# The first stage rewritten: modulation weights as the standing operand, first norms and first products in one order of work

## The reference, cut to what matters

```python
mod = jnp.split((jax.nn.silu(c) @ w_ada[l] + b_ada[l])[:, None, :], N_MOD, axis=-1)
mod_c = jnp.split(jax.nn.silu(c_ctx) @ w_ada[l] + b_ada[l], N_MOD, axis=-1)
...
h_lat = _modulate(_rmsnorm(x, norm1_g[l]), sh1, sc1)      # x: 1024 latent tokens
h_ctx = _modulate(_rmsnorm(ctx, norm1_g[l]), sh1c, sc1c)  # ctx: 256 context tokens
... = jnp.split(h_lat @ w_in, offs, axis=-1)              # and h_ctx @ w_in
```

## Time and profile before

| | us |
|---|---|
| median of 3 runs | 3436.4 (3435.8 to 3438.77) |
| profiled execution | 3435.87, its span 3434.6 |
| TensorE busy | 3270.4 (95%) |
| VectorE busy | 1929.5 (56%) |
| ScalarE busy | 1373.2 (40%) |
| POOL busy | 384.1 (11%) |
| mean granted clock | 0.98 |

### The profile page before, as it was taken

The page is one execution under the profiler, slowest core; times in us unless marked ns, Lnnn a source line. Parts: engine busy times, 40 slices in busy tenths (PEclk is TensorE's granted clock), DMA queues, the critical chain, the costliest instruction groups (busy, mean ns, idle before and its releaser), DMA issues. The chain is left out here.

```text
span 3434.6 us, 39599 instructions
## 1 busy us (share of the span) xinstructions
PE 3270.4 (95%) x14862; PEld 2659.9 (77%) x14862; DVE 1929.5 (56%) x3098; ACT 1373.2 (40%) x2320; POOL 384.1 (11%) x605
## 2 busy tenths in 40 slices
PE   6999999989999999999999999999788899999998
PEld 3888888877788878888888888877555678888886
DVE  4474343454334387777545555655576487777443
ACT  4592232224333244333233356554576343333221
POOL 0121000001100200000010101111211100001011
PEclk8999999999999999999999999999899899999999
DMA  5365433344553423333763433444844523334752
GB/s 218 107 218 183 142 126 123 123 156 157 200 161 117 138 71 117 109 115 118 248 203 97 154 119 137 136 157 150 171 96 104 184 92 117 105 116 165 248 179 77
DMA packets 228045, 494.14 MB, mean 144 GB/s; under 512 B 21520, under 2 KB 84624, under 8 KB 226320
## 3 DMA queue, kind: packets, MB, share of 16 engines
q1 hardware_dynamic: 147728, 302.30, 27.7%
q0 software_dynamic: 80128, 189.30, 16.9%
HBM read 353.63 MB, written 137.89 MB: 143 GB/s over the span
## 5 line engine op out<-in xcount | busy, mean ns | idle before, releaser
L290 PE MATMUL p<-s_xh,s_wh 128*128 128x512 f32 x2256 | 905.6, 401 | 36.9 <-DVE s_tmp L401 12.3
L291 PE MATMUL p<-s_xl,s_wh 128*128 128x512 f32 x2256 | 888.7, 394 | 0.0
L292 PE MATMUL p<-s_xh,s_wl 128*128 128x512 f32 x2256 | 888.2, 394 | 0.0
L290 PEld LDWEIGHTS p<-s_xh,s_wh 128*128 128x128 f32 x2256 | 430.9, 191 | 131.5 <-issue 20.2
L292 PEld LDWEIGHTS p<-s_xh,s_wl 128*128 128x128 f32 x2256 | 429.6, 190 | 92.3
L291 PEld LDWEIGHTS p<-s_xl,s_wh 128*128 128x128 f32 x2256 | 430.6, 191 | 89.6 <-issue 1.7
L2092 PE MATMUL p<-s_xh,s_wh 128*128 128x512 f32 x1152 | 449.5, 390 | 1.1 <-DVE s_xl L2199 1.0
L2094 PE MATMUL p<-s_xh,s_wl 128*128 128x512 f32 x1152 | 448.3, 389 | 0.0
L2093 PE MATMUL p<-s_xl,s_wh 128*128 128x512 f32 x1152 | 448.2, 389 | 0.0
L250 DVE TENSOR_TENSOR s_wl<-s_ws,s_wh 128x1024 fp32r<-128x1024 f32 x157 | 195.3, 1257 | 235.0 <-ACT s_wh L242 234.8
L2092 PEld LDWEIGHTS p<-s_xh,s_wh 128*128 128x128 f32 x1152 | 216.3, 188 | 47.7 <-issue 2.7
(11 more groups left out here) (380 smaller groups left out, 5099.8 us busy)
## 6 DMA issues: line engine op xcount, KB each, us to landing
d_h<-s_fhl POOLq DMA_DIRECT2D x80, 512.0 KB, 3.4
s_ws<-i_Wf SPq DMA_DIRECT2D x48, 512.0 KB, 4.3
s_qb<-i_Wf SPq DMA_DIRECT2D x40, 512.0 KB, 4.1
s_qb<-i_Wf SPq DMA_DIRECT2D x80, 256.0 KB, 3.1
s_ws<-i_Wf SPq DMA_DIRECT2D x80, 256.0 KB, 2.8
s_aw<-i_adaT SPq DMA_DIRECT2D x32, 512.0 KB, 3.7
s_xh<-d_h POOLq DMA_DIRECT2D x16, 1024.0 KB, 12.0
s_xl<-d_h POOLq DMA_DIRECT2D x16, 1024.0 KB, 15.7
```

The lines of the kernel that those rows point to most:

```text
L290: pe.matmul(o, wh, H[:, k, c:c + n], start=(k == 0), stop=False)
L291: pe.matmul(o, wh, L[:, k, c:c + n], start=False, stop=False)
L292: last = pe.matmul(o, wl, H[:, k, c:c + n], start=False, stop=(k == 7))
```

## The change

- `ada_pe`: the weight tile is the standing operand, 16 blocks of 128 columns per k, and the pair of vectors moves (2 columns). Each product writes its own two columns of bank 0 (32 per k); one reduction on VectorE adds the eight up. Row copies and transposes go.
- SP: vector pair and context first, then the tiles of `w_ada` with the four weight tiles between them, then x by halves of 256 KB (all of half 0 before half 1), then `cb`, `WA0`, `cmask` and two more weight tiles. Weight tiles 2 and 3 go to `ACC` and `RB` in place of `WS`, so they need no slot given back.
- The squares of the latent halves have buffers of their own, in the place of `w_ada` tiles, so their first waits for the last of `ada_pe`. They are interleaved on ScalarE with the context's high parts. POOL adds them up.
- TensorE: column sums and spreads of the halves are put into `products_pe` by `mids` (half 0 in the context's group before k = 5 and 7, half 1 in half 0's group before k = 2 and 4). The three groups run in stage 0, and stage 1 begins with the filling products. Half 1's spread is copied to `RB`.
- The banks of the three groups change. The context's keys are copied to `ACC` and stored from there, after POOL's adds.
- `cb` and `WA0` are processed after the second group on ScalarE.

The diff, cut to its core:

```diff
+    ADA = alloc(top, [128, 32], F, "ada")
...
+    def raw_weights(i):
+
+        n = cols_of[i]
+        if 2 <= i < 4:
+            return (ACC, RB)[i - 2][:, 0:n], early_in[i - 2].at(1)
+        return WS[:, i % NS, 0:n], w_in[i % NS].at(i // NS + 1 if i < 2 else i // NS)
...
-            if i >= NS:
+            if i >= 4:
...
+        DIAG = alloc(p0, [128, 1280], F, "diag")
+        DIA = {"c": DIAG[:, 0:256], 0: DIAG[:, 256:768], 1: DIAG[:, 768:1280]}
+
+        adf = AD[:, :, :].rearrange("p a b -> p (a b)")
+        TF = TMP[:, :, :].rearrange("p a b -> p (a b)")
+        SQ = {"c": [TF[:, 256 * k:256 * k + 256] for k in range(8)],
+              0: [adf[:, 8192 + 1024 * k + 512:8192 + 1024 * k + 1024] for k in range(8)],
+              1: [adf[:, 1024 * k + 512:1024 * k + 1024] for k in range(8)]}
...
+        column_bank, spread_bank = {"c": 6, 0: 6, 1: 4}, {"c": 4, 0: 5, 1: 3}
...
-            loads = {2: (0, 1), 3: (2, 3), 4: (4, 5), 5: (6, 7)}
-            for k in range(8):
-                sp.dma_start(AD[:, k, :], D["ada"][k]).then_inc(*ad_in[k].up())
-                if k == 2:
-                    sp.dma_start(XC[:], D["ctxT"]).then_inc(*xc_in.up())
-                for x in loads.get(k, ()):
-                    sp.dma_start(RES[:, x, :], D["xT"][x]).then_inc(*x_in[x].up())
-            weights_sp(NW)
...
-        def ada_pe(k):
-            PEW.wait_ge(*silu.at(1))
-            PEW.wait_ge(*ad_in[k].at(1))
-            for c in range(4):
-                last = pe.matmul(B[c][0:2, :], sc2[:, k, :], AD[:, k, c * 512:c * 512 + 512], start=(k == 0), stop=(k == 7))
-            last.then_inc(*ada.up())
...
-            for k in range(5):
-                ada_pe(k)
-            columns_pe("c")
-            ada_pe(5)
-            spread_pe("c", [])
-            ada_pe(6)
-            columns_pe(0)
-            columns_pe(1)
-            ada_pe(7)
-            spread_pe(0, [rooted.at(1)])
-            spread_pe(1, [rooted.at(2)])
-            PEW.wait_ge(*mcopy.at(4))
-            PEW.wait_ge(*ident_in.at(1))
-            for m in range(16):
-                last = pe.transpose(B[0][:, 2 * m:2 * m + 2], mrow[:, m * 128:m * 128 + 128], ident[0:2, 0:2])
-            last.then_inc(*mturn.up())
-
...
-            for j in range(20):
-                squares_act(j)
-            root("c")
-            for j in range(20, 24):
-                squares_act(j)
-            root(0)
-            root(1)
-            weights_act(NS)
-            ACW.wait_ge(*ada.at(8))
-            for c in range(4):
-                ac.activation(mrow[:, c * 512:c * 512 + 512], B[c][0:2, :], ACT.Copy).then_inc(*mcopy.up())
-            weights_act(NW)
-            modulated_act("c")
-            modulated_act(0)
...
-            for j in range(20):
-                squares_dve(j)
-            inverse_dve("c")
-            for j in range(20, 24):
-                squares_dve(j)
-            inverse_dve(0)
-            inverse_dve(1)
-            weights_dve(NS)
-            mp = B[0][:, 0:32].rearrange("p (m j) -> p j m", j=2)
-            DVW.wait_ge(*mturn.at(1))
-            dv.tensor_tensor(MOD[:, 0:16], mp[:, 0, :], bada, ALU.add).then_inc(*mods.up())
-            dv.tensor_tensor(MODC[:, 0:16], mp[:, 1, :], bada, ALU.add).then_inc(*mods.up())
-            DVW.wait_ge(*mods.at(2))
-            dv.scalar_tensor_tensor(out=GS[:, 0:8], in0=MOD[:, 8:16], scalar=1.0, in1=n1, op0=ALU.add, op1=ALU.mult).then_inc(*mods.up())
-            dv.scalar_tensor_tensor(out=GS[:, 8:16], in0=MODC[:, 8:16], scalar=1.0, in1=n1, op0=ALU.add, op1=ALU.mult).then_inc(*mods.up())
-            DVW.wait_ge(*mods.at(4))
-            modulated_dve("c")
-            weights_dve(NW)
-            modulated_dve(0)
...
+        bank_free[0] = [mods.at(1)]
+        for b in (1, 2, 3):
+            bank_free[b] = []
         firsts = []
         for part, (col, half, n, x, ready) in enumerate(parts(True)):
+            if part == 1:
+                bank_free[6], bank_free[7] = [rooted.at(2)], []
+            if part == 2:
+                bank_free[4], bank_free[5], bank_free[3] = [rooted.at(3)], [shifted.at(16)], [spread_copied.at(1)]
             group = []
             for g, (name, m) in enumerate((("al", 0), ("k", 0), ("k", 1), ("k", 2))):
-                b = ((0, 1, 2, 3), (0, 4, 6, 7), (1, 2, 3, 5))[part][g]
+                b = ((0, 1, 2, 3), (6, 7, 1, 2), (0, 4, 5, 3))[part][g]
                 p = job(name, m, b, col, n, half, x, ready)
                 if name == "al":
                     p.ev = al_lo.at(part + 1)
...
+        def sp_():
+            sp.dma_start(sc2[:], D["cc"]).then_inc(*cc_in.up())
+            sp.dma_start(XC[:], D["ctxT"]).then_inc(*xc_in.up())
+            sp.dma_start(VEC[:], D["vec"]).then_inc(*vec_in.up())
+            sp.dma_start(ident[:], D["ident"]).then_inc(*ident_in.up())
+            for k in range(8):
+                if k in (4, 6):
+                    weights_sp(k - 2)
+                sp.dma_start(AD[:, k, :], D["ada"][k]).then_inc(*ad_in[k].up())
+            for h in range(2):
+                for k in range(8):
+                    sp.dma_start(RES[:, k, 512 * h:512 * h + 512], D["xT"][k][:, 512 * h:512 * h + 512]).then_inc(*x_in[(h, k)].up())
+            sp.dma_start(cb[:], D["crow"]).then_inc(*cb_in.up())
+            sp.dma_start(WA0[:], D["walpha"]).then_inc(*wal_in.up())
+            sp.dma_start(cmask[:], D["cmask"]).then_inc(*cm_in.up())
+            weights_sp(NW + NS)
+
+
+        def ada_pe(k):
+            PEW.wait_ge(*silu.at(1))
+            PEW.wait_ge(*ad_in[k].at(1))
+            for m in range(16):
+                c = 32 * k + 2 * m
+                last = pe.matmul(B[0][:, c:c + 2], AD[:, k, 128 * m:128 * m + 128], sc2[:, k, :], start=True, stop=True)
+            last.then_inc(*ada.up())
...
+        def spread_pe(what):
+            PEW.wait_ge(*diag.at(which[what] + 1))
+            if what == 1:
+                PEW.wait_ge(*spread3_free)
+            pe.matmul(B[spread_bank[what]][:, 0:size[what]], ones[:], DIA[what], start=True, stop=True).then_inc(*spread.up())
+
+        def pe_():
+            for k in range(8):
+                ada_pe(k)
+                if k == 1:
+                    columns_pe("c")
+                if k == 3:
+                    spread_pe("c")
+            products_pe(firsts[0], {5: lambda: columns_pe(0), 7: lambda: spread_pe(0)})
+            products_pe(firsts[1], {2: lambda: columns_pe(1), 4: lambda: spread_pe(1)})
+            products_pe(firsts[2])
...
+        def square_act(what, k):
+            ACW.wait_ge(*(xc_in if what == "c" else x_in[(what, k)]).at(1))
+            if what != "c" and k == 0:
+                ACW.wait_ge(*ada.at(8))
+            ac.activation(SQ[what][k], source(what, k), ACT.Square).then_inc(*squares.up())
...
+        def act_():
+            ACW.wait_ge(*cc_in.at(1))
+            ac.activation(sc2[:, :, :], sc2[:, :, :], ACT.Silu).then_inc(*silu.up())
+            for k in range(8):
+                square_act("c", k)
+            root_act("c")
+            weights_act(NW)
+            for k in range(8):
+                high_act("c", k)
+                square_act(0, k)
+            for k in range(4):
+                square_act(1, k)
+            root_act(0)
+            for k in range(4, 8):
+                square_act(1, k)
+            for k in range(4):
+                high_act(0, k)
+            al_act(0)
+            ACW.wait_ge(*w_lo.at(3))
+            for g, p in enumerate(firsts[0][1:]):
+                ACW.wait_ge(*p.mm)
+                ac.activation(ACC[:, 256 * g:256 * g + 256], B[p.bank][:, 0:256], ACT.Copy).then_inc(*evA.up())
+            for k in range(4, 8):
+                high_act(0, k)
+            root_act(1)
+            ACW.wait_ge(*spread.at(3))
+            ACW.wait_ge(*w_lo.at(4))
+            ac.activation(RB[:, 0:512], B[spread_bank[1]][:, :], ACT.Copy).then_inc(*spread_copied.up())
+            for k in range(8):
+                high_act(1, k)
+            al_act(1)
+            for p in firsts[1][1:]:
+                fill_act_first(p)
+            ACW.wait_ge(*wal_in.at(1))
+            ac.activation(WAL[:, :, :], WA0[:, :, :], ACT.Copy).then_inc(*wal_hi.up())
+            ACW.wait_ge(*cb_in.at(1))
+            ac.activation(cb[:, :], cb[:, :], ACT.Silu).then_inc(*cb_silu.up())
+            al_act(2)
+            for p in firsts[2][1:]:
+                fill_act_first(p)
...
+            inverse_dve("c")
+            weights_dve(NW)
+            sums = ADA[:, :]
+            DVW.wait_ge(*ada.at(8))
+            dv.tensor_reduce(sums, B[0][:, 0:256].rearrange("p (k c) -> p c k", k=8), AX.X, ALU.add).then_inc(*mods.up())
+            mp = sums.rearrange("p (m j) -> p j m", j=2)
+            DVW.wait_ge(*mods.at(1))
+            dv.tensor_tensor(MOD[:, 0:16], mp[:, 0, :], bada, ALU.add).then_inc(*mods.up())
+            dv.tensor_tensor(MODC[:, 0:16], mp[:, 1, :], bada, ALU.add).then_inc(*mods.up())
```

(123 more changed lines are left out.)

231 lines of the change are left out of this document (78 added, 153 removed).

## The result

The changed kernel takes 3459.8 us in the median of four executions (3459.3 to 3461.7) where the kernel before takes 3436.1 (3435.3 to 3438.8): a ratio of 1.0072, 95% interval 1.0059 to 1.0085. It is slower, as forecast, but by 23.7 us instead of 8.4, and above the range of 3437 to 3455. The profiled execution took 3459.89 us with a span of 3458.6, 24.0 more than the span before.

The account below looks back on a forecast made before the run. TensorE, busy 95% of the span, was taken as the bound. Sums, turn, context and latent groups move the third group's end from 127.2 to 135.6 us: +8.4, forecast 3445 us, range 3437 to 3455.

Parts of the forecast that it names:

- What follows: Everything after the third group of first products: claimed to do the same work in the same way, so no change.
- Term 1: Modulation sums: 256 weight loads at the lower clock, 0.215 us each, 55.0 us for eight tiles, from 10.0 to 66.7 us.
- The sign "a granted 0.5": Modulation sums: the granted clock was to show 0.5 until about 73 us.
- Term 2: From the sums to the first context product: 2.8 us with a 0.5 us reduction, so TensorE starts at 69.5 us.
- Term 3: Context's products: about 5 us at the lower clock, then the upper; 0.9 us wait for POOL; end at 86.0 us.
- Term 4: Latent halves' products: waits of 1.2 and 2.0 us, third group's end at 135.6 us including a clock allowance.
- the 0.8 us for the clock: Latent groups: allowance for two close waits bringing the clock down, a third of 2.3 us.
- The first: Rival on the modulation sums: clock rises, loads run 3.9 us a tile, -13.9 us in all, 3422 us; chance 0.16.
- The second: Rival on context and latent groups: POOL's adds take 1.80 us, waits lower the clock twice; +15.7, 3452 us; chance 0.12.
- The third: Rival on context and latent groups: the forecast waits do not appear; +3.5, 3439.9 us; chance 0.11.
- all three waits: TensorE's forecast waits: 0.9 us for POOL in the context group, then 1.2 and 2.0 us at the first latent half.

Follow-up runs that it names:

- e11: The kernel after, unchanged, run again on the same chip as e12: 3459.25 us, ratio 1.0069 to the kernel before.
- e12: The kernel after with its new 128-byte buffer allocated among the first stage's own buffers, same chip as e11: 3447.6 us, ratio 1.0036 to before.
- e2: The kernel before with an unused buffer of 128 bytes a partition where the change allocates its new one: 3448.2 us, ratio 1.0028.
- e7: e1 plus ten passes of 512 columns of ones ahead of the modulation sums' loads: 3448.6 us in one execution.
- e5: e1 with the vector pair moved 64 times over, so each weight load has a product of 128 columns: 3418.6 us, ratio 0.9949 to before.
- e8: e5 plus eight passes on ones ahead, context loaded behind two weight tiles, its sums and spread later, its key copies earlier: ratio 0.9933 to before.
- e1: The kernel after with its new 128-byte buffer allocated among the first stage's own buffers: 3445.95 us, ratio 1.0029 to before.

## Why the prediction was wrong, step by step

**What follows: the step that failed.** "What follows does the same work in the same way, so the forecast is one number" was false. The work is the same; the place of its operands is not. I read the new buffer in the diff as 128 bytes and did not ask what lies behind it. The price is 11.7 us between e11 and e12, and 11.6 between e2 and before. With that term the forecast would have been 3445 + 12 = 3457. The kernel before hints at it only faintly: its large tiles of this kind all lie 128 past; s_uh, 160 past, ran at 230.9 ns (124 products), but s_ul, 160 past as well, at 226.7.

**Term 1: right.** 0.215 us a load, start 10.0 (measured 10.49), end 66.7 (66.94). The rows at 2703 us were the right ones to settle the clock. The sign "a granted 0.5" could not be read off (the column says 1.00); the pace settles it. Two rules of the Trainium skill, TensorE: Matmul & The Clock Gate, were weighed against this term. The load time of 107 ns (section LDWEIGHTS) comes near at the upper level alone (0.111 in e7, 0.113 in e5, 0.116 in e8), with 0.213 at the lower. That activity of the engine releases the throttle (Part 1) does not hold here for loads with products of two columns, which did not lift it (after, and e7 from 12.7 us on); with 128 columns moved under the same loads it does (e5).

**Term 2: right.** The reduction took 0.42 (0.5 taken), the first product came at 69.65 (69.5).

**Term 3: right in sum, a size off.** The clock rose, and POOL is what the column sums waited for; the wait was 1.89 us instead of 0.9. The size that was off is POOL's chain: seven adds took 9.88 us (70.55 to 80.43) instead of 9.0, since they begin 1.43 us apart though each lasts 1.29, and TensorE came 0.3 us before its forecast. I had the duration of single adds; no row had two of these adds directly behind each other. VectorE's slower pace, 1.44 us a k, was not what this wait hung on, as the squares were there before POOL took them.

**Term 4: right, one size off.** Waits 1.68 and 1.98 us (1.2 and 2.0); the first is longer by the low part that took 1.43 instead of 0.75. TensorE took up the third bank at 92.06 us instead of 90.6, 1.5 late, and nothing of the 0.8 us for the clock was spent in this profile: the granted clock stayed at 1.00, so 136.4 us against 135.6. In e11's profile of the same kernel it was 0.50 from 82 to 85 us, and the fill came at 140.73; the allowance was not idle. The fill came at 139.45 (138.6 forecast).

**Rivals.** The first was refused by the clock, and priced rightly (-13.9; e5 -14.1). The second had the right sign: POOL's chain was slower, but by the time between its adds, 0.9 us, and not by their duration (+3.5); the clock fell in these stretches in e11's profile, but not in that of the kernel after. The third did not happen: all three waits are there.

**What stays open.** 9.3 + 11.7 = 21.0 of 24.0 us. The rest I can't place. The stretch of small products between 2420 and 2552 us has +4.3 in this pair of traces, and falls of the clock come at other points in each execution: the same difference dips by 2.7 us at 1201 to 1240 us, and the profiled execution of e1, which has the fast pace, is 14.8 us over before in its span, though its median is 9.4. I did not separate these, nor do the runs show why the address counts.

## What to carry to other kernels

A buffer allocated ahead of other tiles is a change to every product that streams from them: look at the mean distance of starts by moving tile before and after, and keep the large tiles' starts where they were. Where products are so narrow that the load is the work, ask at which level of the clock they will run, and read it from a stretch of the same kernel where such products ran at the lower one. Moving more columns than needed can pay for itself.

## What the runs showed of the hardware

- The pace of products of 512 columns (fp32r) at the upper level changes with the start of the moving operand within 256 bytes: 226.4 to 227.1 ns at 128 past, 225.8 to 231.3 at 192 (one execution), 232.0 to 233.4 at 0, 233.3 at 64 (one execution). Why, the runs don't show, nor whether the standing operand's place matters; it was the same in all of them. Tiles equally far past can differ (at 192, and at 160 in the kernel before), so the start is not all of it.
- 256 loads of 128x128 with a product of two columns each ran at 0.213 us in the kernel after and never came to the upper pace; with a product of 128 columns they did, at 0.113 to 0.116. At the upper level the narrow ones take 0.111 (e7).
- The clock column can say 1.00 over a stretch at the lower pace: 0.213 us a load in the kernel after from 10.4 to 66.9 us, where e7 has the same pace at 0.50.
- POOL's adds of 512 columns, each 1.29 us in the median, begin 1.41 to 1.44 us apart in eleven of thirteen cases (1.68 and 1.69 in the two others).
- Full-width adds on POOL stretch VectorE's operations with two SBUF inputs from 0.48 to 1.12 us (256 columns), from 0.75 to between 1.09 and 1.43 (512) and from 0.69 to 1.75 (the diagonal).
